# A hybrid decoder layer on one core: the mixture and its output product handled in two halves inside each block of queries

## The chip, the cores and the metric

The kernel runs on one core of one Trainium2 chip. The metric is the device time of one execution in microseconds (us). Five engines work side by side: PE (TensorE: matmuls and transposes; PEld are its weight loads), DVE (VectorE), ACT (ScalarE), POOL (GpSimd) and SP (SyncE, which here only issues DMAs). Each engine runs its own instructions strictly in the order in which they are written, and waits on semaphores for the others.

## The reference, cut to what matters

x is 1024 tokens x 1024, all in f32. One projection gives columns for three head groups, whose outputs are gated, put side by side (width 1024) and multiplied by `w_out`; then comes a layer norm.

```
h = x @ w_in                                        # split into the columns of three groups
o_a = rmsnorm(gated_delta_rule(qa, ka, va, g, beta)) * silu(z_a)      # 4 heads x 128: columns 0..511
o_s = (sparse attention over the keys that an indexer selects) * silu(z_s)  # 4 heads x 64
o_m = (attention into 256 memory tokens) * silu(z_m)                  # 4 heads x 64
y = concatenate([o_a, o_s, o_m]) @ w_out
x = layernorm(alpha * x + y) * ln_g + ln_b
```

## The kernel before

**Order of work.** `make_plan()` writes out one list of steps, and every engine walks through this same list and does its own part of each step. So the list is the program order of every engine. There are three stages in it.

*Index stage* (to about 170 us): projections for the indexer, index scores of all blocks of 128 queries.

*Scan stage* (to about 586 us): for each of the four recurrent heads, inverse of the chunk matrices (steps `M`, `XY`, `nw`), then eight steps `scanV`/`scanS` in which PE and DVE hand a state back and forth. Projections (`proj`, `side`: six matmuls of 512 columns each) are woven between them. ACT meanwhile counts scores above a candidate threshold (`count`, L1786), and after six counts DVE works out the next candidate (`update`, L1401 to L1418), 32 rounds in all. Every product of the projections is made of three matmuls, of a high and a low part of each operand. The weights of a group come into a ring of three slots by DMA; the step `split` of a group lets ACT copy the high part (L1703) and DVE subtract to get the low part (L1348). It stands where the group before it begins, eight steps ahead of its first use. For the recurrent head's scan, `scanV` waits for the PSUM bank of an earlier output that DVE adds up (L1328), and its second matmul (L1155) for the state that DVE writes (L1569, L1571). `nw` (ACT copies it out of PSUM) stands after the last `XY`, three work steps later.

*Attention stage* (586 us to the end): eight blocks of 128 queries in the order 3, 4, 2, 5, 1, 6, 0, 7. In this text "block 3" is the first. For block b:
- `sc b h`: scores of head h (PE; DVE adds the mask and takes the maximum L1616, ACT the exponential L1891). They are made one block ahead.
- `msc b i`: memory scores (PE L1198; DVE maximum L1626; ACT four exponentials L1897), two steps at the very end of the block before.
- `pT b k`: four transposes of the probabilities of key tile k; copied out by ACT (even k, L1703) or DVE (odd k, L1630). `lat b k`: latent sum (two f32 matmuls, L1218). `mpT b i`: the same transposes for the memory. `rinv b`: reciprocal of the sums (L1643).
- `o b`: value products (L1237 and L945), scaled by DVE into the right half of `mix` (L1648).
- `deltanet_scale b`: POOL scales the recurrent heads' output (left half of `mix`, brought by SP, L894) (L2040).
- `mixT b i`: four transposes of half i of `mix` (half 0 needs only `deltanet_scale`, half 1 needs `o`), DVE multiplies by the gate (L1660, L1662); then ACT copies the high part of both halves at once (L1703, 1024 columns) and DVE subtracts (`mix_split`, L1652, 1024 columns).
- `y b i s`: the output product; i is the half of the output columns, s = 0..3 takes two of the eight chunks of `mix` each, six matmuls of 512 columns (L1269 to L1271). With s = 3 DVE adds the residual (L1673) and takes statistics (L1675, L1677).
- `rstd b`: ACT works out the inverse deviation (L1919, L1920), POOL refines it in five small steps (L2015, L1946 to L1949). `ln b`: DVE normalises (L1681), POOL multiplies and adds the norm's row (L2046, L2047), SP stores.

The mixture and the output product of a block (all of `mixT`, `mix_split`, `y`) run inside the attention of the next block; the last `y` step closes that block. `rstd` and `ln` of a block come right behind, at the head of the block after. So the last block's mixture and whole output product stand alone at the end. `split out0..7` make the high (ACT) and low (POOL, L2034) part of `w_out` in blocks 3 and 4; `qsplit` (POOL, L2029, L2030) does it for a block's queries, two blocks ahead. PSUM banks are shared in rings: `msc`, `mixT`, `pT`, `mpT` use three banks in turn.

SP issues the loads of a block's queries, gates, recurrent output and residual in a fixed loop over the blocks (L918 to L934).

Of the kernel before, what the change touches and what calls it, by code (L numbers as in the profile page):

```python
# [120 lines left out]
N_LAST_FILLED = 5  # L121
SELECT_RATE = 0.82


def make_plan():
# [128 lines left out]
    for h in range(DNH):  # L254
# [3 lines left out]
        for s in range(LEV0, NLEV):  # L258
# [12 lines left out]
        steps += [*pair("nw", h), 1]  # L271
# [15 lines left out]
    add(("finals",))  # L287

    def attention(b):

        units = [[("pT", b, k)] for k in range(b + 1)] + [[("mpT", b, i)] for i in range(2)]
        units[0].append(("rinv", b))
        for k in range(b + 1):
            units[k + 2].append(("lat", b, k))
# [5 lines left out]
    def second_half(b):  # L300
        return [("y", b, 1, s) for s in range(4)]

    def normalise(b):
        return [("rstd", b), ("ln", b)]
# [10 lines left out]
    for e in [("msc", first_block, 0), ("msc", first_block, 1), ("deltanet_scale", first_block)]:  # L315
        add(e)
    for n, b in enumerate(BLOCK_ORDER):
        queues = [(0, attention(b))]
        if n:
            before = output(BLOCK_ORDER[n - 1])  # L320
            before[2].append(("deltanet_scale", b))
            queues.append((1, before))
        if n > 1:
            for e in normalise(BLOCK_ORDER[n - 2]):
                add(e)
        if n + 1 < NB:
            nb = BLOCK_ORDER[n + 1]
            queues.append((0.5, [scores(nb, h) for h in range(SAH)]))
        if n < 2:

            queues.append((2, [[("split", f"out{i}")] for i in range(4 * n, 4 * n + 4)]))
        for unit in merged(*queues):
            for e in unit:
                add(e)
        if n + 1 < NB:
            add(("msc", nb, 0))
            add(("msc", nb, 1))
        if n + 2 < NB:
            add(("qsplit", BLOCK_ORDER[n + 2]))
        last = second_half(BLOCK_ORDER[n - 1]) if n else []  # L340
        for e in [*last[:3], ("o", b), *last[3:]]:
            add(e)
    for e in [*normalise(BLOCK_ORDER[-2]), *sum(output(BLOCK_ORDER[-1]), []), *second_half(BLOCK_ORDER[-1]), *normalise(BLOCK_ORDER[-1])]:
# [24 lines left out]
def with_splits(plan):  # L368

    groups = group_order(plan)  # L370
    steps, seen, done = [], set(), {e[1] for e in plan if e[0] == "split"}
    for e in plan:
        g = group_of(e)
        if g and g not in seen:
            seen.add(g)
            for ahead in groups[len(seen):len(seen) + 1]:
                if ahead not in done and ahead not in ("mk", "mv"):
                    steps.append(("split", ahead))
                    done.add(ahead)
        steps.append(e)  # L380
    return steps
# [46 lines left out]
def build(nc, x, x_t, mem_t, w_groups, conv_t, dn_a_log, dn_dt_bias, dn_norm_w, kv_norm_w, wuk_r, w_uv, wmem_t, wout_t,  # L428
# [3 lines left out]
    with ctx:  # L432
# [179 lines left out]
        sums, rinv = misc[:, 32:40], misc[:, 40:48]  # L612
# [172 lines left out]
        def _(sp):  # L785
# [128 lines left out]
            sp.dma_start(lnb, ln_b.broadcast_to([P, DM])).then_inc(ln_sem, 16)  # L914
            for n, b in enumerate(BLOCK_ORDER):
                if n + 2 < NB:

                    sp.wait_ge(*filled(("msc", b, 1)))  # L918
                    load_queries(n + 2)
                if n:  # L920

                    sp.wait_ge(*filled(("mixT", BLOCK_ORDER[n - 1], 0)))
                    load_outputs(n)
                if n:
# [1167 lines left out]
```

## Time and profile before

| what | value |
|---|---|
| runs | 861.54, 860.40, 858.76 us; median 860.4 |
| profiled execution | 861.05 us; span 859.2 us |
| mean granted TensorE clock | 0.948 of full |
| PE / PEld busy | 88% / 72% of the span |
| DVE / ACT / POOL busy | 57% / 54% / 21% |
| DMA | 65.86 MB, 23% of 16 engines' span |

The span is what the profiler saw from the first to the last instruction; the execution's own time is 1.85 us longer. An engine's busy share is an average over the stages.

### The profile page before, as it was taken

To read this page: it belongs to the slowest core of one execution; us is meant where nothing else is said; L and a number is where in the kernel's file an instruction comes from. 1 tells how busy PE (TensorE), PEld (TensorE's weight loads), DVE (VectorE), ACT (ScalarE), POOL (GpSimd) and SP (SyncE) were. 2 spreads that over 40 slices of the span, in tenths; PEclk is the share of its full clock that TensorE was granted. 3 is DMA by queue.
4 is the path that set the end of the run, shared out by engine and by line. 5 is a ranking of instruction groups with operands and counts; after the bars stand their busy time and mean duration, and the time that the engine had idled before them with its cause. 6 is when DMAs were issued, how large, how long until landed. Compare 5 with 4: busy or idle time off the path is not lost.

```text
span 859.2 us, 11357 instructions
## 1 busy us (share of the span) xinstructions
PE 754.5 (88%) x3940; PEld 618.8 (72%) x3940; DVE 490.9 (57%) x1068; ACT 461.6 (54%) x1022; POOL 177.6 (21%) x272
## 2 busy tenths in 40 slices
PE   6999969899997899789998899977789889879865
PEld 5888858788886788678986788745666666567553
DVE  5633868846656475554655395885645445454432
ACT  4533566789868875888768832236533223223110
POOL 0000000053111510142111510102653312320320
PEclk9999979989999999999999999998798898998988
DMA  9312110024102330024001341119311311311201
GB/s 355 103 50 75 49 37 26 37 65 115 52 26 65 84 107 25 26 77 129 25 26 61 84 124 62 43 49 323 100 47 58 104 50 56 105 49 38 86 24 50
DMA packets 63912, 65.86 MB, mean 77 GB/s; under 512 B 16368, under 2 KB 49392, under 8 KB 63472
## 3 DMA queue, kind: packets, MB, share of 16 engines
q1 hardware_dynamic: 63856, 65.13, 23.4%
q8 instruction: 32, 0.52, 0.2%
q14 instruction: 24, 0.20, 0.1%
HBM read 48.35 MB, written 16.78 MB: 76 GB/s over the span
## 4 chain that ended last, share of the span: by engine, by line
PE 62%; DVE 14%; ACT 12%; issue 7%; POOL 2%; DMA 2%; SPq 2%; DVEq 0%; ACTq 0%; POOLq 0%
PE bank L953 9%; PE bank L954 9%; PE bank L955 9%; PE bank L945 6%; PE bank L1269 4%; PE bank L1270 4%; ACT cst L1786 4%; PE bank L1271 4%; PE bank L959 3%; PE bank L1218 3%; PE bank L1116 2%; PE bank L1131 2%; PE bank L1129 2%; DVE score L1395 1%; PE bank L1103 1%
## 5 line engine op out<-in xcount | busy, mean ns | idle before, releaser
L953 PE MATMUL bank<-x_hi,ring_split 128*128 128x512 f32 x480 | 199.6, 416 | 8.1 <-DVE x_lo L1344 7.2
L955 PE MATMUL bank<-x_hi,ring_split 128*128 128x512 f32 x480 | 190.6, 397 | 0.0
L954 PE MATMUL bank<-x_lo,ring_split 128*128 128x512 f32 x480 | 190.5, 397 | 0.0
L1786 ACT ACTIVATE cst<-score,sel 128x1024 bf16<-128x1024 f32 (+2 forms) x192 | 166.9, 874 | 25.2 <-DVE sel L1417 25.2
L953 PEld LDWEIGHTS bank<-x_hi,ring_split 128*128 128x128 f32 x480 | 92.5, 193 | 25.0 <-DVE ring_split L1348 7.6
L955 PEld LDWEIGHTS bank<-x_hi,ring_split 128*128 128x128 f32 x480 | 91.9, 192 | 20.3
L954 PEld LDWEIGHTS bank<-x_lo,ring_split 128*128 128x128 f32 x480 | 92.4, 193 | 15.3
L959 PE MATMUL bank<-cst,arena 128*128 128x128 f32 x320 | 52.6, 302 | 23.4 <-ACT arena L1703 6.4
L1269 PE MATMUL bank<-w_out_hi,mix_hi 128*128 128x512 f32 x128 | 61.7, 482 | 12.2 <-DVE mix_lo L1652 12.0
L959 PEld LDWEIGHTS bank<-cst,arena 128*128 128x128 f32 x320 | 42.5, 156 | 35.3 <-issue 9.1
L1965 POOL TENSOR_TENSOR arena<-arena,hsc 128x512 f32<-128x512 f32 x8 | 8.3, 1041 | 277.7 <-ACT arena L1853 277.7
L1348 DVE TENSOR_TENSOR ring_split<-ring,ring_split 128x1024 fp32r<-128x1024 f32 x30 | 39.7, 1323 | 44.3 <-ACT ring_split L1703 44.2
L1703 ACT ACTIVATE arena<-bank 128x512 f32<-128x512 f32 x77 | 44.2, 590 | 36.7 <-PE bank L959 19.8
L1891 ACT ACTIVATE arena<-arena,misc 128x512 f32<-128x512 f32 (+7 forms) x32 | 24.8, 775 | 70.9 <-DVE misc L1622 70.9
L1952 POOL TENSOR_TENSOR arena<-arena,cst 128x512 f32<-128x512 f32 x24 | 32.6, 1381 | 110.3 <-DVE arena L1302 50.0
L1395 DVE SCALAR_TENSOR_TENSOR score<-arena,wis,score 128x384 f32<-128x384 f32 (+3 forms) x70 | 46.1, 658 | 12.4 <-ACT arena L1774 6.4
L1774 ACT ACTIVATE arena<-bank 128x384 f32<-128x384 f32 (+3 forms) x80 | 38.9, 524 | 25.7 <-DVE score L1395 19.7
L1270 PE MATMUL bank<-w_out_lo,mix_hi 128*128 128x512 f32 x128 | 52.6, 411 | 0.0
L1271 PE MATMUL bank<-w_out_hi,mix_lo 128*128 128x512 f32 x128 | 51.6, 403 | 0.0
L1269 PEld LDWEIGHTS bank<-w_out_hi,mix_hi 128*128 128x128 f32 x128 | 25.3, 198 | 27.9 <-DVE mix_lo L1652 17.1
L1218 PE MATMUL bank<-arena,small 128*128 128x512 f32 x72 | 42.4, 674 | 0.0
L945 PE MATMUL bank<-khi,q 128*128 128x384 f32 (+3 forms) x80 | 30.9, 389 | 8.9 <-ACT arena L1774 8.9
(276 smaller groups left out, 1444.4 us busy)
## 6 DMA issues: line engine op xcount, KB each, us to landing
ring<-in_w_groups SPq DMA_DIRECT2D x30, 512.0 KB, 3.4
x_raw<-in_x_t SPq DMA_DIRECT2D x8, 512.0 KB, 9.7
side_z<-stage SPq DMA_DIRECT2D x16, 256.0 KB, 2.0
w_out_sb<-in_wout_t SPq DMA_DIRECT2D x2, 2048.0 KB, 10.8
zgT<-side_z SPq DMA_DIRECT2D x8, 512.0 KB, 3.9
qkvT<-in_x SPq DMA_DIRECT2D x8, 512.0 KB, 4.6
out_y<-arena SPq DMA_DIRECT2D x8, 512.0 KB, 3.0
ring<-in_wmem_t SPq DMA_DIRECT2D x2, 1024.0 KB, 4.7
```

The lines of the kernel that those rows point to most:

```text
L945: last = nc.tensor.matmul(dst, w, r, start=(i == 0), stop=(i == len(pairs) - 1))
L953: nc.tensor.matmul(dst, hi, xh, start=(c == 0), stop=False)
L954: nc.tensor.matmul(dst, hi, xl, start=False, stop=False)
L955: last = nc.tensor.matmul(dst, lo, xh, start=False, stop=(c == KT - 1))
L959: return nc.tensor.transpose(dst, src, ident[0:n, 0:n])
L1218: last = nc.tensor.matmul(ps(key)[:, :], sm[:, kt, 0:P], pTb[(order[e] - 1) % 3], start=(kt == 0), stop=(kt == b))
L1269: nc.tensor.matmul(ps(key)[:, :], mh, wout_hi[:, c, half], start=(c == 0), stop=False)
L1270: nc.tensor.matmul(ps(key)[:, :], mh, wout_lo[:, c, half], start=False, stop=False)
L1271: last = nc.tensor.matmul(ps(key)[:, :], ml, wout_hi[:, c, half], start=False, stop=(c == KT - 1))
L1395: last = v.scalar_tensor_tensor(score[:, at + lo:at + hi], r[:, 0:hi - lo], w, score[:, at + lo:at + hi], ALU.mult, ALU.add)
L1703: return sc.activation(dst, src, ACT.Copy, scale=scale)
L1786: sc.activation(signs[order[e] % 2][:, 0:w], score[:, score_at(b):score_at(b + 1)], ACT.Sign, scale=-1.0, bias=candidate[:, b - 2:b - 1], ...
```

## The change

1. `mixT` and `mix_split` are handled per half: ACT copies 512 columns after each half's `mixT`, and DVE subtracts 512. The y steps are reordered: half 0 of the mixture feeds `y b 0 0`, `y b 0 1`, `y b 1 0`, `y b 1 1`, which now stand inside block b's own attention; `mixT b 1`, `mix_split b 1` and the other four y steps stand in the next block.
2. The memory scores of the next block move from the end to the middle of a block; `rstd` comes right behind the last y step of the block before, and `ln` some steps later. The order of `pT` and `mpT` is turned round, `lat` comes two transposes later, and the row sums get a second buffer.
3. `finals` (last steps of the recurrent heads' norm) moves to the fourth place of block 3. `qsplit 2` moves ahead of `split out0..3`; `deltanet_scale 3` comes behind them. `split out4..7` comes right behind `mixT 3 0`.
4. SP's loop is reordered to match; the first residual load is issued ahead of the loop.
5. The low half of a group's weights is its own step `low`, placed at the fourth step of the group before (where it was the first) for `proj` and `side` groups. `nw` comes right behind the next head's `KB` steps. The exponential table is asked for at the first `sc`.

```
@@ make_plan @@
             if s == NLEV - 1 and more:
-                steps += [*keys_scaled(after)[0], 1.5, *keys_scaled(after)[1], 1.5]
+                steps += [*keys_scaled(after)[0], 1.5, *keys_scaled(after)[1], *pair("nw", h), 1.5]
...
-        units = [[("pT", b, k)] for k in range(b + 1)] + [[("mpT", b, i)] for i in range(2)]
-        units[0].append(("rinv", b))
+        units = [[("mpT", b, 0)], [("mpT", b, 1)], *[[("pT", b, k)] for k in range(b + 1)]]
+        units[min(3, b + 2)].append(("rinv", b))
...
-    def output(b):
-        return [[("mixT", b, 0), ("mixT", b, 1)], [("mix_split", b)], [], *[[("y", b, 0, s)] for s in range(4)]]
+    def half_out(b, i):
+
+        s0 = 2 * i
+        pieces = [[("y", b, c, s0 + s)] for c in range(2) for s in range(2)]
+        return [[("mixT", b, i)], [("mix_split", b, i)], [], *pieces]
...
         if nb is not None:
+            at = [scores(nb, h) for h in range(SAH)]
+            at[1] = [*at[1], *([("qsplit", BLOCK_ORDER[n + 2])] if n + 2 < NB else [])]
+            place = 3 if n else 4
+            at[place:place] = [[("msc", nb, 0)], [("msc", nb, 1)]]
+            queues.append((0.5, at))
...
+            out = half_out(prev, 1)
...
         if n:
+            out[-1].append(("rstd", prev))
+            mine = half_out(b, 0)
+            mine[0].insert(0, ("deltanet_scale", b))
...
+            mine[2].append(("ln", prev))
+            held = mine[-2:]
+            queues.append((1, [*out, *mine[:-2]]))
@@ with_splits @@
+                        late = [("low", ahead)]
+                        if e[0] not in ("proj", "side"):
+                            steps += late
+                            late = []
+            if used == LOW_BEHIND:
+                steps += late
+                late = []
@@ SP @@
+            sp.dma_start(xres, xv[BLOCK_ORDER[0]]).then_inc(xr_sem, 16)
             for n, b in enumerate(BLOCK_ORDER):
                 if n + 2 < NB:
                     sp.wait_ge(*filled(("msc", b, 1)))
+                    sp.wait_ge(*filled(("sc", b, SAH - 1, len(idx_chunks(b)) - 1)))
                     load_queries(n + 2)
                 if n:
...
+                    sp.wait_ge(*released(("mixT", before, 1)))
                     if n + 1 < NB:
                         load_gates(n + 1)
+                    sp.wait_ge(*released(("y", before, 0)))
+                    sp.wait_ge(*released(("y", before, 1)))
+                    sp.dma_start(xres, xv[b]).then_inc(xr_sem, 16)
+                    if n + 1 < NB:
+                        sp.wait_ge(*filled(("mixT", b, 0)))
+                        load_outputs(n + 1)
@@ PE @@
-                    if s == 0:
-                        if i == 0:
-                            pe.wait_ge(mix_split, PLACE[b] + 1)
+                    if i == 0 and s % 2 == 0:
+                        pe.wait_ge(mix_split, order["mix_split", b, s // 2])
@@ DVE @@
-                    v.tensor_tensor(mix_lo[:, :], av(MIXT_AT, DM), mix_hi[:, :].bitcast(F32), ALU.subtract).then_inc(mix_split, 1)
+                    b, i = e[1:]
+                    part = slice(i * 512, (i + 1) * 512)
+                    dve.wait_ge(mix_hi_ready, order["mixT", b, i])
+                    v.tensor_tensor(mix_lo[:, part], mixT[i], mix_hi[:, part].bitcast(F32), ALU.subtract).then_inc(mix_split, 1)
@@ ACT @@
-                    copy(mix_hi[:, :], av(MIXT_AT, DM)).then_inc(mix_hi_ready, 1)
+                    act.wait_ge(*released(e))
+                    copy(mix_hi[:, i * 512:(i + 1) * 512], mixT[i]).then_inc(mix_hi_ready, 1)
```

The lists of `make_plan()` around one boundary of blocks (2 to 5), before and after. Before:

```
... y403 msc50 msc51 qsplit1 y410 y411 y412 o2 y413 | rstd4 ln4 pT50 rinv5 sc100 pT51 mixT20 mixT21 pT52 lat50 mix_split2 sc110 ...
```

After, from the middle of block 2 to the middle of block 5:

```
... msc50 y413 rstd4 pT22 lat20 deltanet_scale2 mixT20 msc51 mix_split20 lat21 ln4 sc530 sc531 y200 lat22 y201 y210 o2 y211 |
mpT50 sc100 mixT21 mpT51 mix_split21 pT50 sc110 qsplit6 pT51 rinv5 y202 sc120 y203 pT52 lat50 y212 pT53 lat51 msc10 y213 rstd2
pT54 lat52 deltanet_scale5 mixT50 msc11 mix_split50 pT55 lat53 ln2 lat54 sc130 y500 lat55 y501 y510 o5 y511 | ...
```

After, in the first block: `... finals sc410 sc411 qsplit2 pT31 rinv3 sc42. pT32 lat30 mpT30 out0 sc43. mpT31 out1 msc40 pT33 lat31 out2 lat32 msc41 out3 lat33 o3 deltanet_scale3 mpT40 mixT30 out4 sc200 mpT41 mix_split30 out5 mixT31 out6 pT40 mix_split31 out7 sc210 qsplit5 y300 ...`.

## Rows read from the trace of the kernel before

**Rows 1.** Page, the chain that ended last, by engine.
```profile
PE 62%; DVE 14%; ACT 12%; issue 7%; POOL 2%; DMA 2%; SPq 2%; DVEq 0%; ACTq 0%; POOLq 0%
```
**Rows 2.** Waits of PE, scan stage, 200 to 500 us: total us, times, longest.
```profile
PE bank L1149 <- DVE o_head L1328: 8.6, 5, 3.1
PE bank L1155 <- DVE dn_s L1569: 8.2, 3, 2.7
PE bank L1171 <- ACT arena L1703: 4.4, 3, 1.5
```
**Rows 3.** Timeline of DVE, 350 to 366 us (start, us, ..., idle before).
```profile
360.63 1.23 DVE L1348 TENSOR_TENSOR ring_split<-ring,ring_split 128x1024 fp32r<-128x1024 f32 x1 [5.63 <-ACT ring_split L1703]
...
362.50 0.15 DVE L1401 TENSOR_TENSOR sel<-sel 128x6 f32<-128x6 f32 x1
...
364.42 0.29 DVE L1561 COPY vnew<-bank 128x128 f32<-128x128 f32 x1
```
**Rows 4.** Timeline of ACT, same stretch.
```profile
354.64 1.15 ACT L1786 ACTIVATE cst<-score,sel 128x1024 bf16<-128x1024 f32 x1 [1.65 <-DVE sel L1417]
```
**Rows 5.** Timelines of DVE (two rows) and ACT, 284 to 302 us.
```profile
285.86 1.23 DVE L1348 TENSOR_TENSOR ring_split<-ring,ring_split 128x1024 fp32r<-128x1024 f32 x1 [2.19 <-ACT ring_split L1703]
...
294.90 0.35 DVE L1571 SCALAR_TENSOR_TENSOR dn_s<-dn_s,sc,bank 128x128 f32<-128x128 f32 x1
...
287.57 0.31 ACT L1710 ACTIVATE junk<-o_head 128x128 f32<-128x128 f32 x1 [1.56 <-DVE o_head L1328]
```
**Rows 6.** Timeline of POOL, first two blocks.
```profile
600.42 1.04 POOL L2040 TENSOR_TENSOR arena<-arena,sc 128x512 f32<-128x512 f32 x1 [6.96 <-DMA arena<-side_o]
601.42 9.30 POOL L2034 TENSOR_TENSOR w_out_lo<-w_out_sb,w_out_hi 128x1024 fp32r<-128x1024 f32 x4
...
611.36 1.26 POOL L2030 TENSOR_TENSOR q_even_blocks_lo<-q_even_blocks,q_hi_even_blocks 128x512 fp32r<-128x512 f32 x1
```
**Rows 7.** Timeline of SP's queue; page, DMA issues (KB each, us to landing).
```profile
599.03 1.28 SPq L831 DMA_DIRECT2D q_even_blocks<-side_q  x2
...
q_even_blocks<-side_q SPq DMA_DIRECT2D x6, 128.0 KB, 3.3
```
**Rows 8.** Timeline of PE: the first matmul of an output product.
```profile
619.08 0.79 PE L1269 MATMUL bank<-w_out_hi,mix_hi 128*128 128x512 f32 x1
```
**Rows 9.** All waits of PE from 638 us to the end.
```profile
PE bank L1269 <- DVE mix_lo L1652: 12.0, 4, 7.4
PE bank L959 <- ACT arena L1703: 6.4, 6, 1.6
PE bank L959 <- DVE arena L1630: 6.2, 3, 2.4
PE bank L945 <- DVE misc L1616: 5.6, 3, 1.9
PE bank L959 <- DVE arena L1660: 2.4, 2, 1.4
```
**Rows 10.** Timeline of DVE at the boundary of blocks 2 and 5.
```profile
670.03 0.69 DVE L1673 SCALAR_TENSOR_TENSOR arena<-qkvT,bank 128x512 f32<-128x512 f32 x1 [0.76 <-PE bank L1271]
...
673.69 0.81 DVE L1681 TENSOR_SCALAR arena<-arena,hsc 128x1024 f32<-128x1024 f32 x1 [2.00 <-POOL hsc L1949]
...
675.78 0.74 DVE L1660 SCALAR_TENSOR_TENSOR arena<-bank,rows,zgT 128x512 f32<-128x512 f32 x1
...
678.30 2.15 DVE L1652 TENSOR_TENSOR mix_lo<-arena,mix_hi 128x1024 fp32r<-128x1024 f32 x1 [1.18 <-ACT mix_hi L1703]
```
**Rows 11.** Timeline of ACT, same boundary.
```profile
672.16 0.58 ACT L1703 ACTIVATE arena<-bank 128x512 f32<-128x512 f32 x1
```
**Rows 12.** Timeline of PE inside block 5: a `pT`, then a `lat`.
```profile
684.64 0.60 PE L959 MATMUL bank<-cst,arena 128*128 128x128 f32 x4
685.07 1.02 PE L1218 MATMUL bank<-arena,small 128*128 128x512 f32 x2
```
**Rows 13.** Windows at half clock from 638 us to 839 us: summed length, then busy us by engine.
```profile
sum 41.00, PE 29.17 PEld 19.12 DVE 27.83 ACT 14.71 POOL 24.33; mean PE 4.86 PEld 3.19 DVE 4.64 ACT 2.45 POOL 4.05
```

More of the change, by code:

```diff
@@ L121 @@
 N_LAST_FILLED = 5
+LOW_BEHIND = 4
 SELECT_RATE = 0.82
@@ L334, in make_plan @@
                 add(e)
[L335 to L343, printed above, removed]
+        for unit in held[:1]:
+            for e in unit:
+                add(e)
+        add(("o", b))
+        if n == 0:
+            add(("deltanet_scale", b))
+        for unit in held[1:]:
+            for e in unit:
+                add(e)
+    for e in [*sum(half_out(last, 1), []), ("rstd", last), ("ln", last)]:
         add(e)
@@ L370, in with_splits @@
     groups = group_order(plan)
-    steps, seen, done = [], set(), {e[1] for e in plan if e[0] == "split"}
+    steps, seen, used, late = [], set(), 0, []
+    done = {e[1] for e in plan if e[0] == "split"}
     for e in plan:
         g = group_of(e)
[L374 to L379, printed above, removed]
+        if g:
+            used += 1
+            if g not in seen:
+                seen.add(g)
+                used = 1
+                for ahead in groups[len(seen):len(seen) + 1]:
+                    if ahead not in done and ahead not in ("mk", "mv"):
+                        steps.append(("split", ahead))
+                        done.add(ahead)
+                        late = [("low", ahead)]
[5 more added lines that the diff above has]
+                late = []
         steps.append(e)
+        if e[0] == "split":
+            steps.append(("low", e[1]))
     return steps
@@ L1344, in _ @@
                     v.tensor_tensor(x_lo[:, t, c, :], x_raw[:, t, c, :], x_hi[:, t, c, :].bitcast(F32), ALU.subtract).then_inc(x_split, 1)
-                elif k == "split" and e[1][:3] != "out":
+                elif k == "low" and e[1][:3] != "out":
                     name = e[1]
-                    dve.wait_ge(weights_hi_ready, order[e])
+                    dve.wait_ge(weights_hi_ready, order["split", e[1]])
                     v.tensor_tensor(w_lo(name), raw(name), w_hi(name).bitcast(F32), ALU.subtract).then_inc(weights_split, 1)
@@ L1726, in _ @@
                     silu_loaded[0] = silu_loaded[0] or k == "silu" or e[1] >= 4 and e[3] == 3
-                elif k in ("gates", "knorm", "GB", "finals"):
+                elif k in ("gates", "knorm", "GB", "sc", "finals"):
                     exp_ln_table()
@@ L2030, in _ @@
                     g.tensor_tensor(q_lo(n), q_raw(n), q_hi(n).bitcast(F32), ALU.subtract).then_inc(head_queries_split, 1)
-                elif k == "split" and e[1][:3] == "out":
+                elif k == "low" and e[1][:3] == "out":
                     name = e[1]
-                    pool.wait_ge(weights_hi_ready, order[e])
+                    pool.wait_ge(weights_hi_ready, order["split", e[1]])
                     g.tensor_tensor(out_piece(wout_lo, name), out_piece(wout, name), out_piece(wout_hi, name).bitcast(F32),
```

87 lines of the change are left out of this document (46 added, 41 removed).

## The prediction

> **What bounds the kernel now.** I read the page first, its chain of waits by engine: PE holds 62% of it, DVE 14%, ACT 12% [rows 1]. PE works through one list in order, so the end moves by the waits of PE that the change takes away or brings, and by the clock around them. Next come PE's waits by stage. In the scan stage three kinds make 21.2 us in three heads: for a PSUM bank that DVE's output addition frees, for the state from DVE, for a bank that ACT's `nw` copy frees [rows 2]. In the attention stage, from the second boundary of blocks to the end, five kinds make 32.6 us, 7.4 of them one wait in the tail, so 25.3 at six boundaries [rows 9]. The timelines of the other engines tell what each wait stands for; the windows at half clock tell what follows.
>
> **Part 1, low halves and `nw`: 9.0 us less.** Two spots per head, each three times.
>
> First spot, the start of a head's scan. `nw` stood behind counts on ACT. Earlier in the list its two copies (0.58 each by [rows 11]) fit where ACT idled 1.65 us [rows 4], so the wait of 1.5 goes. DVE idled 5.63 us for ACT's high half, then spent 1.23 on the low half, and the state behind it came late [rows 3]: the wait of 2.7 goes too. That is 4.4 per head with a wait of 0.2 after it. But I ask what is late next. The next `vnew` on DVE (364.42) stands behind the update of the count (362.50), and this waits for six counts on ACT [rows 3]. ACT works without a pause there; only the two `nw` copies leave the stretch, and with them `vnew` comes 1.1 us earlier, not 4.4. The rest returns as a longer wait for `vnew`. I take 1.1 x 3 = 3.3. Bounds: 0 (the low half, now between two scan steps, costs its 1.23 there) and 4.4 per head.
>
> Second spot, late in a head's scan. DVE waited 2.19 us for ACT's high half and then spent 1.23 [rows 5] ahead of the output addition that frees PE's bank. All it needs is ready before that, so the waits of 3.1, 2.7 and 2.2 go. Behind it, ACT's next counts stood 1.56 us for the same addition [rows 5]; the next update and the state written at 294.90 come earlier by that and no more; with a few tenths of slack at PE, which I put at 0.35, the gain is about 1.9 x 3 = 5.7; bounds 1.2 and 2.7 each.
>
> The weights' low halves, four steps nearer to their use, still have four steps of six matmuls ahead of them. The cover is ACT's high copy being done by then; if it isn't, PE waits for the rest of it. The exponential table comes earlier and costs nothing, ACT having idle time; `finals` likewise (it only feeds `deltanet_scale 3`).
>
> **Part 2, first two blocks: 5.3 us more.** POOL's order there becomes `finals`, `qsplit 2`, `out0..3`, `deltanet_scale 3`, `out4..7`, and PE's `mixT 3 0` stands ahead of the rest of block 4. SP issued the queries of block 2 from 599.03 to 600.3, and they take 3.3 to land [rows 7]; now the residual load (some 0.5 of issue) goes ahead. They land at about 604.0. From there: queries split 1.9 (610.7 to 612.6, copy and subtraction), four low pieces 9.3, `deltanet_scale` 1.0 [rows 6]: 616.3. In the kernel before the pieces began at 601.4 and nothing of PE's hung on `deltanet_scale` after them. ACT's exponentials, copies and four high pieces add up to about 18 us from the stage's start (an estimate from their kinds), so it is done about 606, and POOL is last. PE, behind ACT's copy of the latent sum and its own `o 3`, has run dry by about 609.5. After `mixT` (0.43, as four transposes in [rows 12]) comes the turn: gate 0.75 [rows 10], ACT's copy 0.58 [rows 11], the subtraction at half of 1.23 = 0.6 and three hand-overs of 0.1: 2.3.
>
> Here a row speaks against the change. The subtraction of 1024 columns took 2.15 us at 678.30 [rows 10] beside POOL's multiplications for the norm, and a DVE subtraction of the same size took 1.23 elsewhere [rows 3]. In blocks 3 and 4 both halves now fall beside POOL's unbroken low pieces of 2.3 us each; I book 1.2 for the first half, 0.5 for the second (bounds 0 and 2.3 each). The Trainium skill, page "SBUF — State Buffer", section "Who interferes with whom", says that a VectorE instruction with two SBUF inputs contends with a GpSimd instruction that reads SBUF, and that the later one blocks fully. The trace agrees with it at 678.30. By the rule taken at its worst, each half would wait a whole piece.
>
> So the first output product starts at 616.3 + 0.4 + 2.3 + 1.2 = 620.2, against 619.08 [rows 8]: 1.1 later. And PE has less behind it then: three `pT` and two `lat` fewer, two `mpT` more, 0.4 + 2 x 0.9 = 2.2 us by [rows 12]. A dry stretch of 7 us also leaves PE at half clock until about 623: 1.5. With the 0.5 that is 5.3. Bounds: -2 (queries land a few us earlier) and 9.
>
> **Part 3, boundaries of blocks: 10.9 us more.** What goes: DVE stood 2.00 us at the head of each block for ACT's and POOL's `rstd` chain [rows 10], and behind it the score maximum, the `pT` copy and the gates that free PE. With `ln` moved, the 25.3 us [rows 9] go in full; I book that.
>
> What comes: on POOL, `deltanet_scale` now stands *behind* `rstd`, and PE's `mixT b 0` needs it. The chain after the last y step: DVE's addition starts at 670.03, the refined deviation is there at 673.69 [rows 10], `deltanet_scale` takes 1.04 [rows 6], and a hand-over 0.1: PE may go at 674.85. PE was free at 669.85. That is 5.0 us from y's end to `mixT`. Cover in the new list: a `pT` and a `lat`, 1.3 [rows 12], at four boundaries (blocks 2, 5, 6, 7); nothing at two (1 and 0); one `msc` step, some 0.5, in block 4. Waits: 4 x 3.7 + 2 x 5.0 + 4.5 = 29.
>
> A second one: `mixT` of half 1 stands behind the first score step, and y's second four steps need its split. DVE first does the score maxima (one chunk 0.6, two chunks some 1.9 us), then the gate, an `mpT` copy, the subtraction; PE has only `mpT`, one score step and a `pT` as cover. I get 0.8 where the next block is small (three times) and 1.3 to 1.6 where it is large (three times): 6.8. After `mixT b 0` nearly all is covered: 0.4 in all. Sum 29 + 6.8 + 0.4 - 25.3 = 10.9. Bounds: 3 (no second wait, a shorter chain) and 20 (ACT or DVE lag by 1.3 more at each of seven).
>
> SP's new waits: queries, gates, outputs and residual are each issued at least half a block before use, so nothing hangs on them after block 3. POOL's two passes of `ln` now lie behind `deltanet_scale` and ahead of the next `qsplit`; nobody waits for them.
>
> **Part 4, the clock: 3.1 us more.** After five of six boundary waits the granted clock stood at the lower of its two levels. With the one in the tail the windows at half clock hold 29.2 us of PE work [rows 13]; at half speed half of that, 14.6, is lost, 1.5 of it in the tail, so 13.1 at the boundaries, 2.6 each. The new waits are seven, all 3.7 or longer in one piece. I take six drops of 2.7: 16.2. Bounds -4 and +8.
>
> **Part 5, the tail: 6.1 us less.** The last block's `mixT 7 0` and four y steps are in the attention. `o 7` is covered by a y step; `mixT 7 1` and the turn of 2.3 remain of the wait of 7.4 [rows 9], 5.1 less, and 1.0 of the clock. The norm at the end is as before.
>
> **Sum**: -9.0 + 5.3 + 10.9 + 3.1 - 6.1 = +4.2 us. The profiled execution took 861.05 (span 859.2 and 1.85 around it), 0.65 above the median 860.4: 865.25, or 864.6 against the median.
>
> **The rivals.**
> *Faster, 852* (0.28). Place: the scan stage. If the count chain on ACT gains as much as PE (ACT idled between updates as well, and a count can start earlier once its candidate does), all 21.2 us [rows 2] go instead of 9.0: 864.6 - 12.2 = 852.4. It decides once the scan gives back more than the 13.2 us that parts 2 to 5 cost. For it: DVE's 5.63 us of standing were pure order [rows 3]. Against: `vnew` behind the update.
> *Slower still, 876* (0.22). ACT now holds the memory exponentials, `rstd`, two copies of the mixture and `pT` in one stretch, and `pT` copies stand behind its wait for the statistics. 1.2 us more at seven boundaries and 3 in block 4: 864.6 + 11.4 = 876.
> *The chain is hidden, 820* (0.05). If POOL got `deltanet_scale` done ahead of the statistics, the 29 us and their clock (16) would not come: 864.6 - 45 = 819.6. The list says otherwise: both are POOL's and in this order.
>
> **How the numbers follow.** Forecast 0.45, its own range 857 to 871. A measurement of this kernel tells 0.3% from no change, 857.8 to 863.0. Of the forecast's chance 0.02 lies below, 0.17 inside, 0.26 above. Faster 0.28 + 0.05 + 0.02 = 0.35, same 0.17, slower 0.26 + 0.22 = 0.48. The range 848 to 878 leaves out the last rival and the outer ends of the bounds.
>
> **What would show it.** PE's largest wait in the attention stage should be transposes of L959's kind released by POOL's `deltanet_scale`, seven of 3.7 to 5 us and one of about 7 in block 4; DVE's wait before `ln` should be gone; the subtraction of low halves should no more wait for ACT; a wait for `vnew` of some 3.5 us should stand at each head's second scan step; the tail's wait should be about 2.3. Wrong, if `mixT b 0` doesn't wait for POOL, if the end of the scan stage moves by less than 4 or more than 14 us, or if the clock stays up across the boundaries.

## The result: 878.3 us, 2% slower, and the profile after

The changed kernel takes 878.3 us (median of 4 runs, 877.4 to 879.1), the kernel before 861.0 on the same chip. The ratio is 1.019 with a 95% interval of 1.015 to 1.024. The profiled execution took 878.29, with a span of 876.5 against 859.2: 17.3 us more, where I forecast 4.2.

The first cut of those 17.3 us is by time. The first matmul of an output product starts at 620.78 instead of 619.08 [rows 8], so 1.7 us come before it, and the other 15.6 between it and the end (240.1 us before, 255.7 now). The 15.6 are firm; what lies before the product is not so firm in one trace of each kernel. The kernel with the memory scores apart, below, has the same list up to the attention stage, and its scan stage still ends 1.85 us earlier than that of the kernel before (last matmul at 582.14 and 583.99); in the traces of the changed kernel and of the six others with its scan list it ends between 579.25 and 581.25.

In the attention stage, the waits of PE from 638 us to the end answer to [rows 9] (line, what was waited for, total us, times, longest):

```profile
PE bank L1005 <- POOL arena L2087: 26.7, 7, 4.7
PE bank L1314 <- DVE mix_lo L1698: 10.1, 7, 2.2
```

All five kinds of [rows 9] are gone but for the one on the low half. What came is one kind: the transposes of `mixT b 0` waiting for POOL's scale of the recurrent heads' half (`deltanet_scale`). With the one in block 4 it is eight waits. Three of them in the timeline of PE, and under them the boundary at 741 us in the timelines of the four other engines, SP's rows left out:

```profile
616.09 0.48 PE L1005 MATMUL bank<-cst,arena 128*128 128x128 f32 x1 [11.85 <-POOL arena L2087]
642.68 0.48 PE L1005 MATMUL bank<-cst,arena 128*128 128x128 f32 x1 [3.65 <-POOL arena L2087]
741.15 0.48 PE L1005 MATMUL bank<-cst,arena 128*128 128x128 f32 x1 [4.70 <-POOL arena L2087]
...
736.48 0.69 DVE L1719 SCALAR_TENSOR_TENSOR arena<-qkvT,bank 128x512 f32<-128x512 f32 x1 [0.62 <-PE bank L1316]
...
738.17 0.29 ACT L1966 ACTIVATE hsc<-hsc,misc 128x1 f32<-128x1 f32 x1 [1.26 <-DVE hsc L1723]
...
738.79 0.21 POOL L2062 TENSOR_SCALAR sc<-hsc 128x1 f32<-128x1 f32 x1 [15.72 <-ACT hsc L1967]
...
740.05 1.04 POOL L2087 TENSOR_TENSOR arena<-arena,sc 128x512 f32<-128x512 f32 x1
```

The row to see is POOL's at 738.79: it had stood still for 15.72 us, waiting for the statistics, with the scale behind that wait. The scale itself needs nothing of the statistics.

The clock follows the waits. Windows of the changed kernel at half clock from 638 us to the end of the last boundary, the columns as in [rows 13] but with each window's granted clock, DMA share and GB/s at the end of its row:

```profile
641.50:648.30 6.80, 5.62 (x13) 3.45 (x14) 2.79 (x6) 1.54 (x4) 2.65 (x3) 0.52 0.16 39
...
740.90:751.10 10.20, 9.95 (x22) 6.09 (x23) 4.86 (x11) 2.44 (x7) 2.91 (x3) 0.53 0.11 26
...
sum 36.90, PE 35.31 PEld 21.40 DVE 18.85 ACT 10.34 POOL 8.12; mean PE 5.88 PEld 3.57 DVE 3.14 ACT 1.72 POOL 1.35
```

Six windows, each behind one of the seven waits for POOL (behind the one at 776.09 the clock stayed up), hold 35.31 us of PE work at the lower level (1.2 GHz); half of it, 17.65, is lost. I had 13.1 for before and 16.2 for after.

At the start of the attention stage, SP's queue, POOL's timeline and the issues of this stretch (KB each, median us to landing) answer to [rows 6, 7]:

```profile
595.28 1.48 SPq L870 DMA_DIRECT2D q_even_blocks<-side_q  x2
...
603.88 0.61 POOL L2076 CAST q_hi_even_blocks<-q_even_blocks 128x512 fp32r<-128x512 f32 x1 [13.06 <-issue]
...
605.80 9.23 POOL L2081 TENSOR_TENSOR w_out_lo<-w_out_sb,w_out_hi 128x1024 fp32r<-128x1024 f32 x4
614.99 1.04 POOL L2087 TENSOR_TENSOR arena<-arena,sc 128x512 f32<-128x512 f32 x1
...
q_even_blocks<-side_q SPq DMA_DIRECT2D x2, 128.0 KB, 7.1
```

POOL took up the queries 8.6 us after the start of their issue; I had allowed 5.0, with the residual's issue in it. The four pieces and the scale followed as listed.

In the scan stage, PE's waits from 200 to 500 us answer to [rows 2], and one row of DVE and one of PE to [rows 3]:

```profile
PE bank L1212 <- DVE vnew L1606: 13.4, 6, 3.8
PE bank L1195 <- DVE o_head L1373: 3.1, 5, 1.4
...
361.39 0.17 DVE L1446 TENSOR_TENSOR sel<-sel 128x6 f32<-128x6 f32 x1 [5.46 <-ACT cst L1832]
...
363.67 0.49 PE L1212 MATMUL bank<-vnew,arena 128*128 128x128 f32 x2 [3.80 <-DVE vnew L1606]
```

The three waits of [rows 2] shrank from 21.2 to 3.1, and one for `vnew` grew to 13.4. DVE now stands at the update of the count instead of at the low halves, and the stage's last matmul starts at 579.25 instead of 583.99. Behind the longer waits the clock fell. From 365 to 368 us, behind the wait at 363.67, PE worked without a pause in both kernels, but the granted clock in the changed one was 0.50 and before it was 1.00 (windows of the changed kernel, then of the kernel before):

```profile
365.00:368.00 3.00, 3.00 (x11) 2.53 (x10) 1.65 (x2) 2.98 (x9) 0.00 (x0) 0.50 0.00 0
...
365.00:368.00 3.00, 3.00 (x22) 2.75 (x22) 1.57 (x4) 3.00 (x9) 0.00 (x0) 1.00 0.00 0
```

### The profile page after: what moved, and what is told of

Its sections match the earlier page's. It is cut to its first block, busy times and chain, and to the rows that moved or that the text cites. A ratio compares the mean times of both kernels' runs of the same rounds, so it can differ in the third digit from the quotient of the medians.

```text
span 876.5 us, 11391 instructions
## 1 busy us (share of the span) xinstructions
PE 764.8 (87%) x3940; PEld 623.8 (71%) x3940; DVE 485.4 (55%) x1076; ACT 462.3 (53%) x1029; POOL 184.0 (21%) x272
## 4 chain that ended last, share of the span: by engine, by line
PE 58%; DVE 13%; ACT 13%; issue 9%; POOL 3%; SPq 2%; DMA 1%; DVEq 0%; ACTq 0%; POOLq 0%
PE bank L999 8%; PE bank L1001 8%; PE bank L1000 8%; PE bank L991 6%; ACT cst L1832 5%; PE bank L1314 4%; PE bank L1264 4%; PE bank L1005 4%; PE bank L1315 3%; PE bank L1316 3%; DVE score L1440 2%; PE bank L1162 2%; PE bank L1177 2%; PE bank L1149 2%; PE bank L1244 2%
## 5 line engine op out<-in xcount | busy, mean ns | idle before, releaser
L1005 PEld LDWEIGHTS bank<-cst,arena 128*128 128x128 f32 x320 | 41.2, 153 | 55.4 <-POOL arena L2087 43.5
L1314 PE MATMUL bank<-w_out_hi,mix_hi 128*128 128x512 f32 x128 | 59.7, 466 | 10.1 <-DVE mix_lo L1698 10.1
L1820 ACT ACTIVATE arena<-bank 128x384 f32<-128x384 f32 (+3 forms) x80 | 39.3, 524 | 25.3 <-DVE score L1440 20.7
L1264 PE MATMUL bank<-arena,small 128*128 128x512 f32 x72 | 44.8, 720 | 0.0
L1314 PEld LDWEIGHTS bank<-w_out_hi,mix_hi 128*128 128x128 f32 x128 | 25.0, 196 | 21.4 <-DVE mix_lo L1698 12.1
```

The lines of the kernel that those rows point to most:

```text
L1005: return nc.tensor.transpose(dst, src, ident[0:n, 0:n])
L1264: last = nc.tensor.matmul(ps(key)[:, :], sm[:, kt, 0:P], pTb[(order[e] - 1) % 3], start=(kt == 0), stop=(kt == b))
L1314: nc.tensor.matmul(ps(key)[:, :], mh, wout_hi[:, c, half], start=(c == 0), stop=False)
```

## The experiments

Ten kernels ran, each beside runs of the kernel before on the same chip. Diffs are against the kernel named; the times are medians.

**The order of the scale and `rstd` on POOL**, against the changed kernel:

```
-            out[-1].append(("rstd", prev))
+            out[-3].append(("deltanet_scale", b))
+            out[-1].append(("rstd", prev))
...
-            mine[0].insert(0, ("deltanet_scale", b))
```

> The changed kernel, with the scale of the recurrent half of every block but the first put two output steps ahead of rstd in the list, instead of behind it. Theory A (POOL's order is what makes PE wait): the seven waits of transposes for POOL's scale, 3.40 to 4.70 each and 26.7 us together, go, and most of the half-clock stretches behind them (17.6 us of loss) with them: 878.3 - 26.7 - 12 = about 840. Rival B (DVE and ACT are as late as POOL at those places): the transposes go early, but the output product then waits for the gate behind the statistics, about 2 us at each of seven: 850 to 862. Rival C (the wait named is not the cause): less than 3 us, 875 or more.

It took 843.97, ratio to the kernel before 0.980 (0.977 to 0.983): 34.3 us less than the changed kernel. All of PE's waits from 638 us on are now

```profile
PE bank L1314 <- DVE mix_lo L1698: 14.2, 9, 3.0
```

and the windows at half clock between the blocks are three:

```profile
sum 10.50, PE 10.50 PEld 8.77 DVE 5.65 ACT 4.37 POOL 0.00; mean PE 3.50 PEld 2.92 DVE 1.88 ACT 1.46 POOL 0.00
```

Theory A. Of 26.7 us of waits for POOL nothing is left, 4.1 came back as waits for the low half (10.1 to 14.2), and the clock lost 5.3 instead of 17.65: 26.7 - 4.1 + 12.4 = 35.0. From the first output product to the end it took 220.9 us instead of 255.7, 34.8 less. The product itself starts 3.0 later in this trace (623.76), 2.0 of it already at the end of the scan stage, whose list is the same; so the profiled spans differ by 31.8.

**The queries of block 2**, against the changed kernel:

```
-            at[1] = [*at[1], *([("qsplit", BLOCK_ORDER[n + 2])] if n + 2 < NB else [])]
+            at[1] = [*at[1], *([("qsplit", BLOCK_ORDER[n + 2])] if n and n + 2 < NB else [])]
...
             add(("deltanet_scale", b))
+            add(("qsplit", BLOCK_ORDER[2]))
```

> The changed kernel, with the split of block 2's queries on POOL put behind the four low pieces of the output weight and the first scale, instead of ahead of them. Theory A (POOL stood 13.06 us for the queries and PE's 11.85 us wait at 616.09 hung on it): the four pieces start as soon as ACT's high copies are there, and PE's wait falls to 3 to 5 us; 7 to 9 us less and about 2 of the clock: 868 to 871. Rival B (the four low pieces, 9.3 us, are the bound, and the queries only filled the time before them): 2 us less at most, 876 or more. Something may be given back: the second four pieces then come behind the queries' split.

870.96, 7.4 less than the changed kernel. PE's wait for the scale in block 4 is gone altogether; the first output product starts at 612.07, 8.7 earlier, and what PE still waited for from 590 to 630 us is

```profile
PE bank L1284 <- ACT arena L1750: 3.2, 1, 3.2
PE bank L1245 <- ACT arena L1750: 1.2, 1, 1.2
```

So the queries ahead of the pieces (POOL's standing for them and their split of 1.9 us) were the whole of the wait, and nothing was given back behind it (255.5 us to the end, against 255.7).

**The loads ahead of those queries**, against the changed kernel:

```
-            sp.dma_start(lng, ...)
-            sp.dma_start(lnb, ...)
-            sp.dma_start(xres, xv[BLOCK_ORDER[0]]).then_inc(xr_sem, 16)
...
                     load_queries(n + 2)
+                if n == 0:
+                    sp.dma_start(lng, ...)
+                    sp.dma_start(lnb, ...)
+                    sp.dma_start(xres, xv[BLOCK_ORDER[0]]).then_inc(xr_sem, 16)
```

> The changed kernel, with SP's loads of ln_g, ln_b and the first residual (512 KB each) issued behind block 2's queries instead of ahead of them. Theory A (the 1.5 MB ahead of them makes the queries land 7 to 9 us after their issue, and POOL's low pieces, its first scale and PE's wait of 11.85 us hang on that): the queries are there 4 to 5 us earlier and the first output product starts as much earlier: 878.3 - 4.5 = 874. Rival (they land late because of their own 1 KB and smaller rows, or ACT's high copies are as late): within 1 us, 877 or more.

874.63, 3.7 less; theory A said 4 to 5. The queries, issued at 596.37, were in POOL's hands 3.9 us later instead of 8.6, at 600.27 instead of 603.88, and PE's longest wait for POOL fell from 11.85 to 6.9:

```profile
596.37 1.28 SPq L870 DMA_DIRECT2D q_even_blocks<-side_q  x2
...
600.27 0.61 POOL L2077 CAST q_hi_even_blocks<-q_even_blocks 128x512 fp32r<-128x512 f32 x1 [8.55 <-issue]
```

**The low halves and `nw` alone**, in the kernel before:

```
-                steps += [*keys_scaled(after)[0], 1.5, *keys_scaled(after)[1], 1.5]
+                steps += [*keys_scaled(after)[0], 1.5, *keys_scaled(after)[1], *pair("nw", h), 1.5]
+            elif s == NLEV - 1:
+                steps += [1.5, *pair("nw", h), 1.5]
...
-        steps += [*pair("nw", h), 1]
+        steps += [1]
```

and `with_splits` with the two steps that take the low halves from `split`, as in the change.

> The kernel before, with one part of the change alone: the low halves of the weights moved four steps later and nw moved ahead of the last merge's rest. The prediction said 9.0 us less (852), 1.1 a head at the first spot and 1.9 at the second. The changed kernel's trace has the end of the scan stage 4.7 us earlier: by that 856. Rival (the other parts of the change cost the scan stage something): the part alone gives 9 or more, 852 or less.

858.55, ratio 0.996 (0.994 to 0.998), 2.8 less than the kernel before; the profiled span is 2.9 shorter, all of it before the first output product (616.16). The scan stage's waits are those of the changed kernel:

```profile
PE bank L1182 <- DVE vnew L1577: 13.4, 6, 3.8
PE bank L1165 <- DVE o_head L1344: 3.0, 5, 1.3
```

The last matmul of its scan stage starts at 580.62, inside the 579.25 to 581.25 of the kernels with the whole change. So this part gives some 3 us by itself, and the rest of the change costs the scan stage nothing that can be told.

**Both edits on the lists**, the first and the second together:

> Both edits of the first two kernels together. If they are independent: the sum of their gains, about 840 - 9 = 831 by theory A of each. If the clock or DVE joins them, less than the sum: 835 to 845.

834.84, ratio 0.968 (0.965 to 0.972). The single gains, 34.3 and 7.4, add up to 41.7; together they gave 43.5. They are independent within what the runs can tell.

**The memory scores.** With the waits for POOL taken out, part of the 15.6 us was still unaccounted for: PE's own work had grown. Grouped by kind, the memory-score matmuls stood out. In the kernel before, the two steps of a block are eight records in one go; in the changed kernel they are four and four. Timeline of PE, the kernel before, the row and its successor:

```profile
629.69 1.14 PE L1198 MATMUL bank<-kmT,qmT 64*128 64x256 f32 x8
630.76 0.50 PE L1269 MATMUL bank<-w_out_hi,mix_hi 128*128 128x512 f32 x1
```

and of the changed kernel:

```profile
629.90 1.13 PE L1244 MATMUL bank<-kmT,qmT 64*128 64x256 f32 x4
630.96 0.44 PE L1005 MATMUL bank<-cst,arena 128*128 128x128 f32 x2
```

Eight take 1.07 us, four take 1.06. The two steps read partitions 0 to 63 and 64 to 127; side by side they run at once. Two of the following kernels test this, with something else mixed in, and the third tests it alone. First, against the changed kernel:

```
-            at[place:place] = [[("msc", nb, 0)], [("msc", nb, 1)]]
+            at[place:place] = [[("msc", nb, 0), ("msc", nb, 1)]]
```

> The changed kernel, with the two memory-score steps of every next block side by side in the list, as in the kernel before, instead of apart. In the traces the two steps side by side take 1.07 us as eight records (they read partitions 0 to 63 and 64 to 127); in the changed kernel each of them takes 1.06 alone, as four records. Theory A (side by side the two run at once on TensorE, apart they don't): six times about 1.0 us less, less what of it had covered a wait: 878.3 - 5 = 873. Rival (the longer time is the hand-over behind any step, whatever stands there): no change, 877 or more.

869.19, 9.1 less. From the first output product to the end it is 245.4 us against 255.7, 10.3 less: the extra PE time, six times 1.06 = 6.4, and 4.7 of the waits for the low half, less 1.1 more for POOL:

```profile
PE bank L1005 <- POOL arena L2087: 27.8, 7, 4.8
PE bank L1314 <- DVE mix_lo L1698: 5.4, 7, 2.2
```

The gain in the waits I had not expected, and it isn't the pair's. `make_plan()` merges its queues by the share of each that is done, so a queue with one unit less shifts its neighbours. In this list `mixT b 1` stands ahead of the next block's first score step in five blocks where it stood behind it, for block 5 so (the changed kernel, then this one):

```
o5 y511 mpT10 sc600 sc601 mixT51 mix_split51 ...
o5 y511 mpT10 mixT51 sc600 sc601 mix_split51 ...
```

The waits of those output products for the low half, of block 5 in the changed kernel and here:

```profile
727.66 0.50 PE L1314 MATMUL bank<-w_out_hi,mix_hi 128*128 128x512 f32 x1 [2.06 <-DVE mix_lo L1698]
...
724.97 0.50 PE L1314 MATMUL bank<-w_out_hi,mix_hi 128*128 128x512 f32 x1 [0.30 <-DVE mix_lo L1698]
```

Where the next block is large (its scores come in two chunks), the three waits fell from 1.56, 2.06 and 2.14 to 0.53, 0.30 and 0.24: these are the 4.7. Where it is small they stayed (0.73 and 0.67 before, 0.72 and 0.69 after). The merge moved other steps by a place or two as well, so this is read from the lists and rows, and no kernel shifts `mixT b 1` alone. By it the pair itself has about 6.4 of the 10.3 us. The first output product starts 2.0 later in this trace, 1.6 of it at the end of the scan stage.

Second, the same edit on the kernel with both edits:

> The kernel of e4_both (834.8) with the two memory-score steps side by side. Theory A: with PE's waits for POOL gone, nearly all of the 6.4 us is on the path: 834.8 - 5.5 = 829. Rival: the time comes back in the waits of the output product for the low half of the mixture, 14.9 us in e4_both: 833 or more.

821.89, 13.0 less; more than theory A said, and again with the shifted steps: the waits for the low half fall from 14.9 to 11.0 us. The profiled spans differ by 12.4, of which 2.6 lie before the first output product. But two of its six pairs behind that point did not overlap, at full clock. The first pair and a later one in the timeline of PE, then ACT's copy of the transposes ahead of it and the weight loads of the pair's second step:

```profile
623.24 1.14 PE L1245 MATMUL bank<-kmT,qmT 64*128 64x256 f32 x8
...
655.13 2.26 PE L1245 MATMUL bank<-kmT,qmT 64*128 64x256 f32 x8
...
655.63 0.58 ACT L1750 ACTIVATE arena<-bank 128x512 f32<-128x512 f32 x1
...
656.26 0.73 PEld L1245 LDWEIGHTS bank<-kmT,qmT 64*128 64x128 f32 x4 [0.41 <-ACT arena L1750]
```

The list here reads `pT 2 2`, `mixT 2 0` and then the pair, and steps of this class take three PSUM banks in turn, so the pair's second step gets the bank of `pT 2 2`. ACT, with the deviation's two steps in front, has copied that one at 656.21, when the first step of the pair was just over (655.13 + 1.06), and the second step's weight load waited 0.41 us for this copy. The other slow pair, at 682.67, has the same rows. At 708.57 the same place in the list has its bank free at 707.91 (an odd tile, copied by DVE), and the pair takes 1.07. That the bank is the cause is my reading of these rows; no kernel tried it.

Third, the opposite edit in the kernel before, which never had the fault:

```
             add(("msc", nb, 0))
-            add(("msc", nb, 1))
...
-        for e in [*last[:3], ("o", b), *last[3:]]:
+        apart = [("msc", nb, 1)] if n + 1 < NB else []
+        for e in [*last[:1], *apart, *last[1:3], ("o", b), *last[3:]]:
```

> The kernel before, with the second memory-score step of each next block put one output step behind the first, instead of side by side with it, and nothing else. Theory A: seven times 1.0 us of TensorE time more, 6 to 7 us: 867. Rival (no work of two at once; order only): within 1 us of the kernel before, 861.

868.89, ratio 1.008 (1.005 to 1.012): 7.2 slower than the kernel before, with one step of a block moved by one place and no other. In PE's order the two steps come apart in six blocks; block 4's stay together, so theory A's term is 6 x 1.06 = 6.4 and not seven times 1.0. In the traces it is 8.5 us more from the first output product to the end (248.6 against 240.1); the 2 us beyond the pairs I have not traced. A four-record row of it follows an eight-record row of the same place in the kernel before (693.00):

```profile
694.11 1.13 PE L1198 MATMUL bank<-kmT,qmT 64*128 64x256 f32 x4
```

**`vnew` behind the update of the count**, against the last version but one (both edits and the pair):

```
+    for h in range(DNH):
+        a, z = plan.index(("scanS", h, 0)), plan.index(("scanV", h, 1))
+        updates = [i for i in range(a, z) if plan[i][0] == "update"]
+        if updates:
+            late = [e for e in plan[updates[0]:z] if e[0] in ("update", "count")]
+            rest = [e for e in plan[updates[0]:z] if e[0] not in ("update", "count")]
+            plan[updates[0]:z + 1] = [*rest, plan[z], *late]
```

> e6_both_memory_pair, with the update of the count that stood between the first and the second scan step of each head, and the counts behind it, moved behind the second scan step. Theory A (the wait of 3.80 us for vnew, three times, is only the order on DVE: vnew stands behind the update, which waits for six counts on ACT): the three waits fall to 1 us or less and the scan stage ends 6 to 9 us earlier: 829 - 7 = 822. Rival B (the count chain on ACT is the bound of the scan stage: whatever PE gains there, it waits for later): the waits go, and come back at the next updates or at the end of the selection: 827 to 830. Rival C: counts start later, the chain of counts gets longer and the kernel slower, 832.

816.84, ratio to the kernel before 0.947 (0.944 to 0.950), the best of all. The waits from 200 to 500 us:

```profile
PE bank L1220 <- DVE vnew L1614: 8.2, 8, 1.7
PE bank L1203 <- DVE o_head L1381: 5.0, 6, 1.3
```

The longest is 1.7 instead of 3.80, and the scan stage's last matmul starts at 573.41 instead of 579.58, 6.2 earlier, in the range that theory A gave. The medians differ by 5.1, the profiled spans by 6.1. The waits alone don't make it: 13.4 us of them fell to 8.2 where theory A's three waits would have left 5.0, and those for the output addition grew by 2; that is some of rival B. The clock has room for the rest. The kernel that it starts from has a stretch at the lower level behind each of the three longest waits (granted clock 0.89, 0.94 and 0.94 in the windows of 30 us from 260, 350 and 440), and here the granted clock is 1.00 in every window of 30 us from 200 to 590.

**The second wait, for the low half of the mixture**, against that version:

```
+    for b in BLOCK_ORDER[1:-1]:
+        i, z = plan.index(("mixT", b, 1)), plan.index(("mix_split", b, 1))
+        a = i
+        while plan[a - 1][0] == "sc":
+            a -= 1
+        plan[a:z + 1] = [*plan[i:z + 1], *plan[a:i]]
```

> e8_state_before_update (816.8), with the transposes and the split of the second half of the mixture moved ahead of the first score step of the next block. Theory A (the second wait, 0.7 us where the next block is small and 2.1 where it is large, is DVE doing the score maxima first): the six waits for the low half of about 7.5 us together fall to about 2: 812. Rival (DVE has the same work in either order, and the score maxima, then the exponentials and pT, come late instead): 816 to 818.

817.99, against 816.84. But this kernel tests nothing: the edit moves no step. It looks for a score step right in front of `mixT b 1`, and in the list that it starts from there is none (`mpT10 mixT51 sc600 ...`), because the memory pair had shifted `mixT b 1` ahead of the score steps already. Both kernels walk the same 1223 steps. So the 1.2 us between them, and the 0.6 between their waits for the low half (10.4 and 11.0 us, ten pieces each), are what two sets of runs of one list differ by; the median of all ten runs is 817.3. What its theory A said is answered, as far as the rows go, by the memory pair in the changed kernel above: where the next block is large, most of the wait went with the shift; where it is small, none did. What makes the small waits stays open.

## Why the forecast was 13 us too low

The sign and the largest wait were forecast, the size was not: 864.6 against 878.3, and that lies 0.3 us above the upper end of my range. The forecast said 7.9 us less before the first output product and 12.1 more behind it; it came to 1.7 more and 15.6 more.

**Part 1, -9.0: measured -2.8 alone.** The step that failed is the first spot, "1.1 x 3 = 3.3". The wait of 3.5 for `vnew` that I forecast came, 3.80 three times; the gain booked beside it did not. The second head's scan in the timeline of PE, in the kernel before and then in the changed kernel: work before its first spot, a scan step between its two spots, work behind its second spot.

```profile
336.26 1.95 PE L1116 MATMUL bank<-arena 128*128 128x128 f32 x16
...
370.97 0.28 PE L1171 MATMUL bank<-vnew,arena 128*128 128x128 f32 x1
...
407.54 1.73 PE L1116 MATMUL bank<-arena 128*128 128x128 f32 x14
...
335.47 1.95 PE L1162 MATMUL bank<-arena 128*128 128x128 f32 x16
...
371.48 0.28 PE L1217 MATMUL bank<-vnew,arena 128*128 128x128 f32 x1
...
404.12 1.95 PE L1162 MATMUL bank<-arena 128*128 128x128 f32 x16
```

The changed kernel is 0.8 us ahead, then 0.5 behind, then 3.4 ahead: 1.3 lost at the first spot, 3.9 gained at the second. Over the three heads it lost 3.0 at the first spots, where I had booked a gain of 3.3, and gained 7.8 at the second, where I had booked 5.7. Against the other trace with the old scan list (the memory scores apart) it is 2.9 and 8.1, and the kernel with this part alone lost 4.7 and gained 7.6. Single spots differ by up to 2 us between traces, the sums by less. The loss has two parts. `vnew` comes 1.1 us earlier on the time axis, as I said (363.32 for 364.42, second head), but PE comes to it earlier still and doesn't keep its lead. And the standstill of 3.8 us costs clock: 3 us at 0.52 and 0.50 behind it in the first two heads (in the third the kernel before had such a stretch too), for which part 1 had no term, though part 4 had one for waits as long. Behind all of it stand ACT's counts. The waits of DVE for ACT's high halves are gone, but most of that time comes back at the update, from 200 to 500 us:

```profile
DVE ring_split L1348 <- ACT ring_split L1703: 29.1, 13, 5.6
DVE sel L1401 <- ACT cst L1786: 14.7, 11, 2.0
...
DVE sel L1446 <- ACT cst L1832: 32.5, 13, 6.1
```

43.8 us of waiting before, 32.5 after. Moving `vnew` ahead of the update, the experiment on `vnew`, takes the three standstills and their clock away. That part 1 as a whole came out only 6.2 too good was luck: the surplus at the second spots hid a third of the miss at the first.

**Part 2, the queries.** I took the landing of 3.3 us from [rows 7], which is the median of six such loads over the kernel. This load stands behind 1.5 MB in one queue. In the kernel before, the same burst had its own row, which I had not asked for:

```profile
q_even_blocks<-side_q SPq DMA_DIRECT2D x2, 128.0 KB, 5.8
```

With the residual ahead it is 7.1. That is 3.6 of the 9.6 us missed ahead of the first product; the scan stage's smaller gain is 4.3 (9.0 less 4.7, by the one trace of each). Of the remaining 1.7, 1.0 is the queries' issue, which starts at 595.28 where 599.03 less 4.7 is 594.3, and 0.7 the rest of that chain: from the cast to the first product 16.9 us, forecast 16.2. The contention booked for the first low half (1.2) didn't come: POOL stood still when it began. The second half paid 0.46, booked at 0.5. Timeline of DVE in blocks 3 and 4, then POOL's two pieces beside them:

```profile
619.34 0.68 DVE L1698 TENSOR_TENSOR mix_lo<-arena,mix_hi 128x512 fp32r<-128x512 f32 x1
...
621.71 1.14 DVE L1698 TENSOR_TENSOR mix_lo<-arena,mix_hi 128x512 fp32r<-128x512 f32 x1 [1.08 <-ACT mix_hi L1749]
...
619.68 2.62 POOL L2081 TENSOR_TENSOR w_out_lo<-w_out_sb,w_out_hi 128x1024 fp32r<-128x1024 f32 x1 [3.65 <-ACT w_out_hi L1749]
622.24 2.88 POOL L2081 TENSOR_TENSOR w_out_lo<-w_out_sb,w_out_hi 128x1024 fp32r<-128x1024 f32 x1
```

These rows fit the rule that the prediction cites, that the later instruction blocks. The second half began at 621.71, when POOL's first piece had some 0.5 us to go, and took 0.46 longer. POOL's two pieces began while DVE was at a low half, and took 2.62 and 2.88 where the shortest of its kind took 2.34. What the rule doesn't say is the worst case that I took from it, a whole piece: the later one waits for what is left of the earlier one.

**Part 3, boundaries.** Waits for POOL: forecast 29.0, measured 26.7. The second waits: forecast 6.8, measured 10.1 - 2.17 (tail) = 7.9; the reason given for the larger ones, DVE's score maxima in front, fits the shift in the memory-pair kernel. The 25.3 went in full. Sum +9.3 for a forecast of +10.9.

**Left out: the memory scores, +6.4.** This is the term that I put at nothing, and the largest single miss behind the first product. I took such a step as cover of 0.5 and gave moving it no price. The kernel before showed the row, eight records in 1.07, and I read it as two steps of 0.53. The price of one alone, 1.06, stands in no row of before; but the operand, 64 partitions, was there to be read. The Trainium skill, page "TensorE: Matmul & The Clock Gate", section "Part 3: Packing small matmuls — row/col tiling", says that matmuls of fewer than 128 rows run at the same time when they lie in different row groups. The trace agrees with its numbers (1.07 for eight, 1.06 for four); it speaks against this change, and I did not weigh it.

**Part 4, clock:** +3.1 forecast, 17.65 - 13.1 = +4.5 measured. Right kind, too small: six windows as forecast, of 5.9 us of PE's work in the mean where I had 5.4.

**Part 5, tail:** -6.1 forecast. The wait fell from 7.4 to 2.17, and the clock's share there hardly (2.70 us at half clock, 1.35 lost, for 1.5): -5.4. From the traces alone; no kernel isolated it.

Parts 3 to 5 with the memory scores make 9.3 + 6.4 + 4.5 - 5.4 = 14.8 of the 15.6; the other 4.2 that I had put behind the first product for blocks 3 and 4 came to 0.8.

**The rivals.** "The chain is hidden, 820" said what takes the waits away, and the first experiment made it true by one line: 34.3 us for the 45 I gave it. "Faster, 852" needed 13.2 us from the scan stage; it gave 4.7 in the changed kernel's trace and 2.8 alone. "Slower still, 876" has nearly the measured time and the wrong mechanism: it wanted the waits at the boundaries 1.2 us longer than forecast, and they were 0.3 us shorter each. Its 3 us more in block 4 did come (11.85 for about 7), but by the queries and not by ACT.

## What to carry to other kernels

When a step is moved, look for what stands ahead of it on its in-order queue that it doesn't need: here two items of a list in the wrong order cost 34 us, twice what the change as a whole cost. Before steps are spread apart, look whether they shared an engine while side by side. And after an edit to a generated list, compare the lists step by step: one edit here moved more than it said, and one moved nothing. Done so, the change's idea is worth having: with three edits to the order of the list the same work takes 821.9 us instead of 861, and with the fourth, which is about the scan and not about the change's idea, 816.8. The fourth was not tried in the kernel before.

## What the hardware did that I had not expected

Two TensorE steps on the two halves of the partitions take 1.07 us side by side and 2 x 1.06 with one output step between them; side by side in the list was not always enough, two pairs took 2.19 at full clock. PE's clock fell from 1.00 to 0.50 behind single standstills of 3.8 us in the scan stage, and was at 1.00 in the same places where the longest was 1.7. DVE and POOL held each other up only for what was left of the other's instruction: 0.46 us of DVE's, 0.28 and 0.54 of POOL's. And a 128 KB load took 3.9 us from the start of its issue until its use behind one load of 256 KB, and 8.6 behind that and three of 512 KB in the same queue.
